# The low half of a weight unit in one VectorE instruction instead of two, for the experts' down projection

## The reference, cut to what matters

```python
def swiglu(x, w1, w3, w2):
    return (jax.nn.silu(x @ w1) * (x @ w3)) @ w2

def moe_swiglu(x, router_w, w1, w3, w2):
    ...
    top_vals, top_idx = lax.top_k(logits, TOP_K)          # 2 of 8
    gates = jax.nn.softmax(top_vals, axis=-1)
    ...
    for e in range(N_EXPERTS):
        out = out + combine[:, e:e + 1] * swiglu(xt, w1[e], w3[e], w2[e])
```

## Time and profile before

| | us |
|---|---|
| median of 3 runs | 1906.88 |
| lowest and highest | 1901.38 and 1907.42 |
| the profiled execution | 1906.07 |
| its span (first to last instruction) | 1904.3 |
| `wlo` instructions of 128x1024 from 840 to 1870 us: 672, mean 1.219 | 774.8 |
| idle time of DVE in front of these | 33.4 |
| distance of two rounds (PE's first matmul of the scatter, 1104.60 and 1230.19) | 125.59 |

### The profile page before, as it was taken

One profiled execution on the slowest core, in us unless ns is written; L12 is line 12 of the kernel. 1 busy time (PEld: TensorE's weight loads), 2 busy tenths in 40 slices (PEclk: granted clock), 3 DMA queues, 4 the chain that ended last, 5 costly groups with the idle time before them and its releaser, 6 DMA issues.

```text
span 1904.3 us, 26803 instructions
## 1 busy us (share of the span) xinstructions
PE 1812.1 (95%) x9562; PEld 1545.7 (81%) x9562; DVE 1394.7 (73%) x1653; ACT 1219.2 (64%) x1536; POOL 5.9 (0%) x13
## 2 busy tenths in 40 slices
PE   8999979989999989869999999999999999999997
PEld 7877768979998779768888878788788787887885
DVE  4466755755665466558989899898998998989984
ACT  5546545644443355537778777687877777878773
POOL 0000000000000000000000000000000000000000
PEclk9899989999999999969999999999999999999999
DMA  9752223425445344318989899899898998998980
GB/s 325 250 182 95 80 97 133 155 97 197 177 177 204 128 170 165 113 46 325 378 314 374 328 360 368 327 359 377 319 368 324 357 374 322 371 353 339 367 330 23
DMA packets 68336, 483.32 MB, mean 254 GB/s; under 512 B 7610, under 2 KB 7738, under 8 KB 10928
## 3 DMA queue, kind: packets, MB, share of 16 engines
q1 hardware_dynamic: 66480, 475.26, 65.6%
q0 software_dynamic: 1792, 7.18, 1.8%
HBM read 478.22 MB, written 4.19 MB: 253 GB/s over the span
## 4 chain that ended last, share of the span: by engine, by line
PE 75%; DVE 11%; issue 7%; ACT 7%; DMA 0%; DVEq 0%; ACTq 0%; POOLq 0%
PE ps L1483 18%; PE ps L1484 18%; PE ps L1488 18%; DVE wlo L904 6%; PE ps L1728 4%; PE ps L1735 4%; PE ps L1729 4%; ACT whi L561 3%; PE ps L1466 3%; PE ps L1940 1%; PE ps L1941 1%; ACT xgh L858 1%; DVE sg L1027 1%; ACT sg L684 1%; PE ps L1831 1%
## 5 line engine op out<-in xcount | busy, mean ns | idle before, releaser
L904 DVE TENSOR_TENSOR wlo<-raw,whi 128x1024 fp32r<-128x1024 f32 x906 | 1044.0, 1213 | 168.3 <-ACT whi L561 167.8
L561 ACT ACTIVATE whi<-raw 128x1024 fp32r<-128x1024 f32 x906 | 903.4, 1055 | 140.9 <-PE ps L1488 118.8
L1483 PE MATMUL ps<-whi,xgh 128*128 128x512 f32 x896 | 355.5, 397 | 4.6 <-ACT whi L561 4.6
L1484 PE MATMUL ps<-whi,xgl 128*128 128x512 f32 x896 | 349.9, 391 | 0.0
L1488 PE MATMUL ps<-wlo,xgh 128*128 128x512 f32 x896 | 277.5, 391 | 0.0
L1483 PE MATMUL ps<-whi,xh 128*128 128x512 f32 (+1 forms) x448 | 188.0, 420 | 21.1 <-issue 9.8
L1483 PEld LDWEIGHTS ps<-whi,xgh 128*128 128x128 f32 x896 | 169.0, 189 | 38.4 <-ACT whi L561 4.8
L1488 PEld LDWEIGHTS ps<-wlo,xgh 128*128 128x128 f32 x896 | 168.8, 188 | 35.8
L1484 PEld LDWEIGHTS ps<-whi,xgl 128*128 128x128 f32 x896 | 169.1, 189 | 33.3
L1484 PE MATMUL ps<-whi,xl 128*128 128x512 f32 (+1 forms) x448 | 182.7, 408 | 0.0
L1483 PE MATMUL ps<-whi,mTh 128*128 128x512 f32 x448 | 175.7, 392 | 0.0
(11 more groups left out here) (288 smaller groups left out, 1895.7 us busy)
## 6 DMA issues: line engine op xcount, KB each, us to landing
raw<-in_w_moe_dram SPq DMA_DIRECT2D x336, 1024.0 KB, 7.1
raw<-in_w_fixed_dram SPq DMA_DIRECT2D x112, 1024.0 KB, 4.9
bias_scratch<-revb POOLq DMA_DIRECT2D x1, 3072.0 KB, 38.3
bias<-bias_scratch POOLq DMA_DIRECT2D x1, 2048.0 KB, 16.8
raw<-in_w_fixed_dram SPq DMA_DIRECT2D x4, 512.0 KB, 4.2
tok<-in_xt_dram SPq DMA_DIRECT2D x2, 512.0 KB, 4.6
h<-in_x_dram SPq DMA_DIRECT2D x1, 1024.0 KB, 13.9
out_dram<-h SPq DMA_DIRECT2D x2, 512.0 KB, 2.7
```

Source lines behind the costliest of these rows:

```text
L561: AC(whi[:, v % SPL, c], raw[:, v % RAW, c], ACT.Copy).then_inc(high_done, 1)
L904: V.tensor_tensor(wlo[:, v % SPL, c], raw[:, v % RAW, c], whi[:, v % SPL, c].bitcast(F32), ALU.subtract).then_inc(low_done, 1)
L1483: mm(o, hi(k0 + k, T), wh[:, k, :], start=first and k == 0, stop=False)
L1484: mm(o, lo(k0 + k, T), wh[:, k, :], start=False, stop=False)
```

## The change

DVE's `split_to` makes the low half of a unit in one instruction of 2048 columns if the unit is one of the 14 of w2 in a round, and in two of 1024 otherwise: in all other stages of the kernel, and in units 0 to 27 of a round. The merged instruction waits for both high halves of its unit and adds 2 to `low_done` when it is done. The programs of the other engines are as they were, so PE's two waits for the low halves of such a unit are released together.

```diff
--- before.py
+++ after.py
@@ -898,11 +898,13 @@
                 while g.split <= u:
                     v = g.split
                     n = unit_columns(v, g.post)
-                    for half in range(2):
-                        dve.wait_ge(high_done, g.at(high_done, 2 * v + half + 1))
-                        c = slice(half * n // 2, (half + 1) * n // 2)
+                    down = v >= U["ffn1"] and not g.post and (v - U["ffn1"]) % UNITS_ROUND >= 4 * NFB
+                    parts = 1 if down else 2
+                    for part in range(parts):
+                        dve.wait_ge(high_done, g.at(high_done, 2 * v + (2 // parts) * (part + 1)))
+                        c = slice(part * n // parts, (part + 1) * n // parts)
                         V.tensor_tensor(wlo[:, v % SPL, c], raw[:, v % RAW, c], whi[:, v % SPL, c].bitcast(F32),
-                                        ALU.subtract).then_inc(low_done, 1)
+                                        ALU.subtract).then_inc(low_done, 2 // parts)
                     g.split += 1
 
             def invert_root(k):
```

## The result

The changed kernel takes 1914.25 us (median of 14 runs, 1907.35 to 1920.40), the kernel before 1904.96 us (median of 14 runs). The ratio is 1.0043, with a 95% interval from 1.0029 to 1.0057: slower by 0.43%, 8.2 us. (The two medians are 9.3 us apart and the two means 8.0; 8.2 is what the ratio gives.) The forecast was 1910.0 us, 3.1 us more than before, in a range from 1903 to 1915. The direction was right and the size too small, and the likeliest case (within 0.3%) is not what came.

What follows compares the result with a forecast made beforehand. PE's matmul stream was taken as the bound, waiting for DVE at `pick` and `yl`. 0.81 us late less 0.42 won back leaves 0.39 a round, times 8 is 3.1 us: 1910.0 us, own range 1906 to 1913, 8-in-10 range 1903 to 1915.

Steps and rivals of the forecast that it cites:

- the likeliest case: Measured time within 0.3% of the kernel before, given a chance of 0.75.
- What a merged unit takes: A 2048-column VectorE instruction lasts 2.29 us, 2.20 from start to start against 2.27 for two halves, saving 0.07 us.
- Units 28 to 31 without cost: In the down projection, `ht` and `mTl` come slightly later, and nothing of the delay reaches PE.
- `pick` late by 0.81 us: Before the gather, merged units 32 to 35 move `pick` from 1202.58 to 1203.39, and all three engines by 0.81 us.
- this is the one place where the new wait is not hidden: Merged unit 32 waits for ACT's second half and starts 0.94 us late.
- 0.42 us won back: Behind the gather, six merged units take 13.20 us instead of 13.62, so 0.39 of the 0.81 us delay stays.
- units 36 to 41 run free: Behind the gather, these six merged units follow at 2.20 us each without waiting for ACT.
- The stall at unit 36 costs nothing: PE stalls about 0.40 us for unit 36's low part, covered by the `yl` wait, which shrinks from 1.38 to 0.56.
- the delay kept whole: Rival, chance 0.19: a larger stall at unit 36 loses the win-back; 6.5 us slower, or 8.2 if merged instructions don't overlap.
- The transfers: Loads released later by merged units still land in time, the tightest wanted 8.9 us later; cost nothing.
- DVE as the bound: Rival, chance 0.06: the new wait costs nothing and 0.98 us a round comes off PE's waits; 7.8 us faster, 1899.1.
- the fixed part saved whole: Rival, chance 0.09: each merged unit saves 0.15 us, units 36 to 41 win back 0.90; 1.4 us less, 1905.5.

## Why the prediction came out as it did

**What a merged unit takes: right.** 2.29 us long, 2.20 from start to start, 0.07 saved. The rule of the fixed part, in the Trainium skill (VectorE: DVE Perf Modes, the section on the TRN2 errata), gives the length exactly, and the distance of starts again shows less than the whole of it: 2.20 us against twice 1.136, and six merged units bring 0.31 us and not 0.9.

**Units 28 to 31 without cost: right,** by the run with these alone.

**`pick` late by 0.81 us: the size nearly right, its cause too narrow.** It is 0.92 us. The step "this is the one place where the new wait is not hidden" was wrong. Unit 32 alone and unit 35 alone each make `pick` late by 0.91 to 0.92 us, 33 and 34 together by 0.52. That the four together cost no more than unit 32 was so in the sum too, which is why the size came out nearly right. I had looked for ACT's second half against the *merged* timeline, where the delay of unit 32 has already made room for the next ones. Part of the missing 0.1 us is the start behind ACT: 0.02 us in my sum (in the earlier trace rows, 1193.46 to 1193.49), 0.10 us measured (1201.91 to 1202.01, 1202.95 to 1203.05).

**0.42 us won back: right in kind, 0.31 measured.** The step that failed is that units 36 to 41 run free. Unit 36 does. Unit 41 is held by ACT by about 0.08 us, because PE's stall at unit 36 moves `half_used` and with it ACT's halves; I had followed that stall to the halves of the next round's units and to `yh`, and not to this one.

**The stall at unit 36 costs nothing: right.** PE takes the low part 1215.28 - 1204.83 = 10.45 us after the gather's first matmul instead of 10.05, 0.40 late as in the sum (the waits row counts 0.21 of it as idle, as a matmul of 512 columns is listed with 0.39 us where the next starts after 0.23), and with the restart the half units behind it stand 0.53 us late; the wait for `yl` went from 1.38 to 0.53 us (0.56 in the sum) and covered it. The second `yl` waited 0.19 us for `yh` and PE did not notice. The first rival, the delay kept whole because the stall eats the margins, is therefore not what happened, although its 6.5 to 8.2 us are near the 8.2 measured. That 1914.25 us lies in the range of 1903 to 1915 is luck in this sense: its upper end was there for this rival, and the forecast's own range ended at 1913. The transfers did cost nothing: no engine waits for one in the rounds.

**Clock: the step that is missing, a term of the sum that stood at nothing.** The prediction carried PE's later start of the gather forward as a shift, with every matmul behind it at its old distance. The delay kept and the time won back alone come to 0.61 us a round, 4.9 us, where 3.1 were forecast. The rest, 3.3 us by the ratio and 4.4 by the medians, fits one or two rounds with a fallen clock; the profile has two. The kernel with the idle time filled has the 4.9 us (5 us by the ratio of 1.0027) and no fall in its profile, and delaying `pick` without merging anything brings falls on. I had no rival for it, and the rows of before could have suggested one only by its absence: the wait for `yl`, 1.38 us, has never brought the clock down in the loop, in any of these kernels. What follows it are matmuls of 512 columns; the gather's have 128.

**Neither of the other rivals.** DVE as the bound would have made the change faster, and the fixed part saved whole would have won back 0.90.

**What stays open.** Which rounds lose their clock is settled by the place of the beat. The Trainium skill (TensorE: Matmul & The Clock Gate, the part on the gate) says that the chip's look at the activity runs free of the kernel, and that the moment of a change depends on where in it the first matmul lands. The traces agree: the beat stays the same through a whole execution, and the fall comes 1.24 to 2.72 us into the gather in the ten rounds that have one. Not shown is how much idle time it takes between 0.40 us, which never did it, and 1.30; nor whether the small matmuls have a share in it besides the idle time; nor how many rounds fell in the runs without a profile.

## What to carry to other kernels

Merging two instructions saves a part of their fixed cost and gives away the head start of the first half; where the engine follows its supplier closely, the second is the larger (0.92 us against 0.07), and the delay lands on whatever stands next in that engine's queue. Ask of each such result who waits for it, and check the wait of every merged instruction against the supplier's unmerged timeline, each by itself. If a small result that another engine wants (`pick`) stands behind a long run that nobody is short of, move it ahead of the run: that was worth 0.35% here, more than any merge, and made the merge harmless.

## What the runs showed of the hardware that was not expected

An idle time of PE of 1.30 to 1.60 us in front of matmuls of 128 columns let the granted clock fall from 2.4 to 1.2 GHz in 9 of 40 rounds, all those in which the clock's own beat had a step 1.24 to 2.72 us behind the first of these matmuls; one of 1.00 us did so in 1 of 8. A fall cost 2.7 us up to the scatter in the changed kernel; where units 36 to 41 are not merged it cost 2.1 us, with 0.2 us more up to the next gather where another round follows. An idle time of 0.39 or 0.40 us in the same place never did it, in 13 rounds with such a step, nor one of 1.38 us in front of matmuls of 512 columns. And a merged VectorE instruction that waited for the second of two ScalarE instructions started 0.10 us after its end, one of the old form that waited for the first 0.03 us; whether the half waited for or the longer form makes the difference is not shown.
